# w_down in seven block products for eight: all four column groups and all 44 tiles, with the residual read and the sums joined near the end

## The reference

```python
h = rmsnorm(x, ffn_norm[l])
gate = jnp.einsum('bsd,df->bsf', h, w_gate[l])
up = jnp.einsum('bsd,df->bsf', h, w_up[l])
x = x + jnp.einsum('bsf,fd->bsd', jax.nn.silu(gate) * up, w_down[l])
return rmsnorm(x, final_norm)
```

## Time and profile before

| | us |
|---|---|
| median of 3 runs | 1979.49 |
| lowest and highest run | 1979.39, 1980.06 |
| span of the profiled execution | 1977.3 |
| first matmul of w_down | 1512.65 |
| last matmul starts | 1969.47 |

### The profile page before, as it was taken

One profiled execution on the slowest core, in us unless ns is written; L12 is line 12 of the kernel. 1 busy time (PEld: TensorE's weight loads), 2 busy tenths in 40 slices (PEclk: granted clock), 3 DMA queues, 4 the chain that ended last, 5 costly groups with the idle time before them and its releaser, 6 DMA issues.

```text
span 1977.3 us, 29282 instructions
## 1 busy us (share of the span) xinstructions
PE 1967.3 (99%) x10300; PEld 1691.6 (86%) x10300; DVE 1654.7 (84%) x2386; ACT 1126.6 (57%) x2064; POOL 167.2 (8%) x261
## 2 busy tenths in 40 slices
PE   9999999999999999999999999999999999999998
PEld 7888888888888988888888888888888888888886
DVE  8877767777766999999999999999998688697886
ACT  6566666666346655555646555555556355566643
POOL 5002333223100000000000000000000000000000
PEclk9999999999999999999999999999999999999999
DMA  9322222224334344443434344444347836546433
GB/s 343 127 83 70 70 71 70 69 70 139 102 117 138 119 148 137 130 139 130 137 132 142 131 134 135 136 139 135 132 138 238 303 120 227 176 148 221 126 130 133
DMA packets 132889, 276.16 MB, mean 140 GB/s; under 512 B 13392, under 2 KB 13424, under 8 KB 131744
## 3 DMA queue, kind: packets, MB, share of 16 engines
q1 hardware_dynamic: 120896, 239.65, 37.9%
q0 software_dynamic: 6640, 23.82, 3.1%
q10 hardware_dynamic: 5232, 11.04, 1.6%
HBM read 242.99 MB, written 31.46 MB: 139 GB/s over the span
## 4 chain that ended last, share of the span: by engine, by line
PE 96%; DVE 2%; issue 1%; DMA 1%; ACT 0%; SPq 0%; POOLq 0%; POOL 0%; DVEq 0%; ACTq 0%
PE bank L841 25%; PE bank L844 13%; PE bank L702 7%; PE bank L768 7%; PE bank L770 7%; PE bank L769 7%; PE bank L704 7%; PE bank L703 7%; PE bank L900 3%; PE bank L898 3%; PE bank L899 3%; PE bank L925 2%; PE bank L942 1%; PE bank L910 1%; PE bank L909 1%
## 5 line engine op out<-in xcount | busy, mean ns | idle before, releaser
L841 PE MATMUL bank<-s_two,t_hi 128*128 128x512 f32 x2352 | 557.3, 390 | 0.0
L1485 ACT ACTIVATE t_hi<-t_raw 128x1792 fp32r<-128x1792 f32 x176 | 302.5, 1720 | 358.1 <-DVE t_raw L2155 269.7
L841 PEld LDWEIGHTS bank<-s_two,t_hi 128*128 128x128 f32 x2352 | 433.5, 188 | 84.7
L2161 DVE TENSOR_TENSOR t_lo<-t_raw,t_hi 128x1792 fp32r<-128x1792 f32 x176 | 355.7, 2021 | 20.7 <-ACT t_hi L1485 20.6
L844 PEld LDWEIGHTS bank<-s_two,t_lo 128*128 128x128 f32 x2352 | 298.9, 191 | 10.4 <-DVE t_lo L2161 0.6
L844 PE MATMUL bank<-s_two,t_lo 128*128 128x256 f32 x2352 | 302.1, 283 | 0.4 <-DVE t_lo L2161 0.4
L1136 ACT ACTIVATE w_hi<-raw 128x512 fp32r<-128x512 f32 x268 | 168.8, 631 | 189.5 <-PE bank L770 141.4
L1778 DVE TENSOR_TENSOR w_lo<-raw,w_hi 128x512 fp32r<-128x512 f32 x268 | 184.6, 690 | 56.6 <-ACT w_hi L1136 56.0
L2152 DVE TENSOR_TENSOR t_raw<-t_raw 128x1024 f32<-128x1024 f32 x176 | 215.0, 1221 | 17.2 <-DMA t_raw<-in_w_gu 15.5
L702 PE MATMUL bank<-h_hi,w_hi 128*128 128x512 f32 x416 | 166.0, 399 | 1.1 <-DVE h_lo L1782 0.6
L704 PE MATMUL bank<-h_lo,w_hi 128*128 128x512 f32 x416 | 162.6, 391 | 0.0
(11 more groups left out here) (260 smaller groups left out, 3487.8 us busy)
## 6 DMA issues: line engine op xcount, KB each, us to landing
t_raw<-in_w_gu SPq DMA_DIRECT2D x348, 256.0 KB, 2.8
raw<-in_w_down SPq DMA_DIRECT2D x112, 256.0 KB, 3.6
raw<-in_w_in SPq DMA_DIRECT2D x104, 256.0 KB, 2.7
gu_mid<-part POOLq DMA_DIRECT2D x43, 512.0 KB, 2.9
gu_next<-gu_mid SPq DMA_DIRECT2D x36, 512.0 KB, 6.9
raw<-in_w_out SPq DMA_DIRECT2D x64, 256.0 KB, 3.0
fast_y<-in_w_down SPq DMA_DIRECT2D x24, 512.0 KB, 5.0
fast_z<-in_w_down SPq DMA_DIRECT2D x16, 512.0 KB, 4.7
```

Source lines behind the costliest of these rows:

```text
L841: mm = nc.tensor.matmul(b[:, :], t_hi[r][:, ti, q, :], both, start=d == 0 and q == 0, stop=d == DOUBLES - 1 and q == 1 and i < 4, skip_gro ...
L1485: nc.scalar.activation(t_hi[r][:, :, :, :].rearrange("p a q c -> p (a q c)"), t_raw[r][:, 1:8, :, :].rearrange("p a q c -> p (a q c)"), AC ...
L2161: nc.vector.tensor_tensor(t_lo[r][:, :, :, :].rearrange("p a q c -> p (a q c)"), t_raw[r][:, 1:8, :, :].rearrange("p a q c -> p (a q c)"), ...
```

## The change

All of w_down now goes by seven block products. There are two pairs of column groups: (0, 2) with h = 0 and (1, 3) with h = 1. Chunk 0 has 4 tiles (2 near, 2 far) and chunks 1 to 5 have 8, together 44. A unit is (chunk c, product p, depth u, pair h), 256 rows by 512 columns and 12 matmuls as before; a chunk has 7 x 2 x 2 = 28 units, chunk 0 has 14. The order of the products is P1, P5, P6, P7, P3, P4, P2.

- Removed: the plain units, their splits on ACT and DVE, their adds to `x_res`, the last 4 tiles' part.
- Every product's sums stay in `m_sum`, now 14 buffers for 7; a product takes four banks, and `keep` and `seed` move four.
- The high and low parts of weights have rings of 4 (before 2): ACT may start `f_high` of the unit three ahead when unit v-1 is off the banks' list (`f_used`).
- DVE's loop does, for unit v: `f_sum` of v+4, gate operations of the next chunk (slots of `GATE_SLOT`), `f_low` of v+3.
- SP reads z again in P3, after `f_low` of the same unit, and P4's `f_sum` takes it.
- The residual is read in chunk 5, at P3's first unit, into the place where gate tiles lay; joins and adds follow in `ending`.
- The last product, P2 of chunk 5, is done pair by pair, and the last pair by position block. Rows 256 to 511 are finished first.

```diff
-CHUNK = 8
-CHUNKS = (TILES - 4) // CHUNK
...
+P1, P5, P6, P7, P3, P4, P2 = range(FAST)
+SUMMED_W, SUMMED_A = (P5, P6, P7, P4), (P5, P6, P7, P3)
+FAST_FROM = "yxxyzxz"
+CHUNKS = 6
+ENDING = CHUNKS - 1
+DEPTHS = (1,) + (2,) * ENDING
+F_RING, A_RING = 4, 4
+F_AHEAD, SUM_AHEAD = 3, 4
...
+GATE_SLOT = ({4: 2, 5: 3, 6: 4, 7: 5, 0: 6, 1: 7, 2: 8, 3: 9}, {4: 4, 5: 6, 6: 8, 7: 10, 0: 14, 1: 16, 2: 18, 3: 20})
...
+            if p == P3:
+                sp.wait_ge(f_lo_done, v + 1)
+                load_block("z", c, u, h, 1, 0)
...
+            if (c, p, u, h) == (ENDING, P3, 0, 0):
...
+                for n in range(NC):
+                    sp.wait_ge(x_moved[n], X_SPILLED)
+                    sp.dma_start(x_res[:, :, 512 * n:512 * (n + 1)],
...
+            if v >= F_RING:
+                act.wait_ge(f_used, v - F_RING + 1)
+            nc.scalar.activation(flat(f_hi[v % F_RING]), flat(fast_raw[FAST_FROM[p], u][h]), ACT.Copy).then_inc(f_hi_done, 1)
...
         silu(0, 0)
         silu(0, 1)
...
+        act.wait_ge(t_used, ALL_T - 2)
+        f_high(0)
+        f_high(1)
+        act.wait_ge(t_lo_done, ALL_T)
+        a_high(ITEMS[0])
+        silu(0, 4)
+        silu(0, 5)
         take_products(7, 1, 0, 5)
...
+            if e == 20:
+                for h in range(2):
+                    dve.wait_ge(joined, h + 7)
+                    add_block(sum_of(P5, h), 1, h + 2, r2_sign, 0)
...
+        def fast_slot(v):
+
+            c, e = UNITS[v][0], v - FIRST_UNIT[UNITS[v][0]]
+            if v + SUM_AHEAD < len(UNITS):
+                f_sum(v + SUM_AHEAD)
+                for item in items_at(v + SUM_AHEAD):
+                    a_sum(item)
+            if c < ENDING:
+                for k, slot in GATE_SLOT[c > 0].items():
+                    if e == slot:
+                        gate_scaled(c + 1, k)
+                    if e == slot + 2:
+                        gate_times_up(c + 1, k)
+            if v + F_AHEAD < len(UNITS):
+                f_low(v + F_AHEAD)
+                for item in items_at(v + F_AHEAD):
+                    a_low(item)
+            if v == 1:
+                post(7, 1)
+            if c == ENDING:
+                ending(e)
```

More of the change, by code:

```diff
@@ L256, in build @@
[L256 to L269, removed]
+    place_d = place_s
+    g_near = sb("g_near", [P, 4, 2, SEQ], at=place_d)
@@ new lines, in build @@
+    g_far = [sb(f"g_far{i}", [P, 4, 2, SEQ], at=place_d + 16384 * (i + 1)) for i in range(2)]
+    x_res = sb("x_res", [P, NT, D], at=place_d)
+    places_f = (place_w + 8192, place_w + 16384, place_s4 + 16384, place_s4 + 24576)
+    f_hi = [sb(f"f_hi{r}", [P, 2, SEQ], F32R, at=at) for r, at in enumerate(places_f)]
+    f_lo = [sb(f"f_lo{r}", [P, 2, SEQ], F32R, at=at + 4096) for r, at in enumerate(places_f)]
+    places_a = [place_x + 24576 + 4096 * r for r in (2, 3, 0, 1)]
+    a_hi = [sb(f"a_hi{r}", [P, 2, HALF], F32R, at=at) for r, at in enumerate(places_a)]
@@ L418, in unit_of @@
[L418 to L451, removed]
+    def a_source(c, p, u):
+        near, far = g_near[:, 2 * u:2 * u + 2, 0, :], g_far[c % 2][:, 2 * u:2 * u + 2, 0, :]
+        if p == P1:
+            return near[:, :, 0:HALF]
+        if p == P4:
+            return far[:, :, HALF:SEQ]
+        if p == P2:
+            return far[:, :, 0:HALF]
+        return g_far[c % 2][:, 2 * u + (p == P7), 1, :].rearrange("p (k c) -> p k c", c=HALF)
@@ new lines, in fast_unit @@
+        def fast_unit(v, halves=range(2)):
+            c, p, u, h = UNITS[v]
+            if 0 in halves:
+                pe.wait_ge(f_lo_done, v + 1)
+                pe.wait_ge(a_lo_done, ITEM[c, p, u] + 1)
+                if u == 0 and c > 0:
+                    pe.wait_ge(seeded, seeded_count(c, p, h))
+                elif u == 0 and p == P1:
+                    pe.wait_ge(bank_taken, taken_by(0, TILES - 2) + 4 * (h + 1))
+                elif u == 0 and p == P5:
+                    pe.wait_ge(bank_taken, taken_by(0, TILES - 1))
+                elif u == 0:
+                    pe.wait_ge(kept, kept_count(c, p - 2, h))
+            rf, ra = v % F_RING, ITEM[c, p, u] % A_RING
+            for tp in halves:
+                for i in range(2):
+                    ah, al = a_hi[ra][:, i, P * tp:P * (tp + 1)], a_lo[ra][:, i, P * tp:P * (tp + 1)]
+                    mm = three(bank_of(c, p, h, tp)[:, :], ah, al, f_hi[rf][:, i, :], f_lo[rf][:, i, :],
+                               c == 0 and i == 0, u == DEPTHS[c] - 1 and i == 1)
+            return mm
@@ L1738, in _ @@
+        f_high(2)
+        a_high(ITEMS[1])
         take_products(7, 1, 5, QUAD)
[L1739 to L1751 removed]
@@ L2534, in _ @@
[L2534 to L2541 removed]
+        f_low(0)
@@ new lines, in _, with gain @@
+        a_low(ITEMS[0])
+        gate_scaled(0, 4)
+        gate_scaled(0, 5)
+        f_low(1)
+        gate_times_up(0, 4)
+        gate_times_up(0, 5)
+        f_sum(2)
+        a_sum(ITEMS[1])
+        f_sum(3)
+        f_low(2)
+        a_low(ITEMS[1])
+        for v in range(len(UNITS) - 2):
+            fast_slot(v)
+        def gain(n):
+            cols = slice(512 * n, 512 * (n + 1))
+            nc.vector.tensor_tensor(o_fin[:, n, :], x_res[:, 1, cols], g_fin[:, cols], ALU.mult).then_inc(gained, 1)
@@ L2544, in _ @@
+        finish_mean(0, 7, 5, 3)
+        dve.wait_ge(added, C11_LEFT + 4)
+        gain(1)
+        dve.wait_ge(sq_done, FIRST_SQ + 16 + 8)
+        dve.wait_ge(total_done, 7)
+        nc.vector.tensor_scalar(mean[:, 1:2], sums[:, 1, 2:3], 1.0 / D, mean_rest[:, 0:1], ALU.mult, ALU.add).then_inc(mean_done, 1)
+        for i in range(2):
+            finish_row(0, slice(1024 * i, 1024 * (i + 1)), 6)
     @block.gpsimd
```

855 lines of the change are left out of this document (320 added, 535 removed).

## The result

| | before | after |
|---|---|---|
| median of the runs, us | 1979.55 | 2032.64 |
| lowest and highest run | 1979.39, 1980.06 | 2032.09, 2033.90 |
| span of the profiled execution | 1977.3 | 2030.3 |
| first matmul of w_down | 1512.65 | 1515.76 |
| end of the last matmul | 1969.86 | 2010.86 |

The ratio is 1.0269 (95% interval 1.0256 to 1.0282). The sign and the cause were forecast; the loss was forecast at 33.5 us and is 53, outside the range.

A forecast was written before the change was run, and what follows sets the result against it. DVE was taken to become the bound of w_down, 433 us for PE's 419. 1977.3 - 38.1 + 19.3 (chunk 0) + 21.7 (chunks 1 to 4) + 16.2 (chunk 5) + 14.5 (end) = 2010.9, with 2.2 for the median 2013; range 1992 to 2024.

The forecast's parts named there:

- Which engine bounds: w_down stage: DVE has 433 us of work for PE's 419, so DVE bounds even without waits.
- Rivals A: w_down stage: PE stays the bound, 1941, or 1949 with DVE's sum as the limit; chance 0.04.
- rival B: w_down stage: DVE bounds but reads land in time, 1987, half of it 1965 to 1995; chance 0.15.
- signs named: w_down: DVE 90% or more; three PE idles over 5 us in first 55; f_hi waiting at chunk ends.
- Start: w_down's first unit: starts at 1514.2, after copies out of the last gate tile's banks, a 1.6 us term.
- large terms: Chunk 0: PE stalls of 5.6, 5.7 and 5.2 us, from DVE's early work and late z reads.
- small terms: Chunk 0: three slots carry 2.9 to 3.5 us of DVE work for 2.72, 1.2 us more.
- rival D: As the forecast, but the clock falls in long stalls or x_res is slower: 2018 to 2028; chance 0.21.
- Chunks 1 to 4: PE stalls 7.6 us in chunk 1, then 4.7 each: 2.6 early slots, 1.4 later slots and z, 0.7 signals.
- Chunk 5: 16.2 us of PE stall: DVE waits 6.8 for z behind residual reads, then has 32.3 of work.
- The tail: After the last matmul: DVE's list and output writes, end 21.6 us after PE, 14.5 more than before.
- lower end of the mechanism: All reads landing at once takes 8.8 off chunk 0, 5.3 chunks 1 to 4, 6.8 chunk 5, 5 end: 1985.

The follow-up runs named there:

- z early: Changed kernel with y and z swapping roles, P4's far block read four units sooner, the gain's read moved: 1994.55 us, ratio 1.0074.
- spread: On z early, gate operations moved to slots 12 to 15 and 18 to 22, the last gate tile's post to unit 8: 1982.27 us.
- the earlier start: On the post split, gate operations of chunk 0's far tiles put ahead of its first low parts, silus likewise: 1979.74 us.
- the post split: On spread, the last gate tile's post cut in two, at units 8 and 11: 1979.85 us, ratio 1.0004.
- half reads: Changed kernel with only gate, not up, read for the near tiles of chunks 2 to 5: 2020.92 us, ratio 1.0212.
- The residual read behind z: Changed kernel with the four residual reads issued after P3's last z read instead of its first: 2025.95 us, ratio 1.0237.

## Why the prediction was wrong, step by step

- **Which engine bounds: right.** Rivals A and B fell. PE's 168 matmuls less were right, DVE's durations too (73.4 us of work in a chunk for 72.8). Three of the signs named did not come: DVE was busy 86% and not 90%, PE sat for over 5 us twice in the first 55 us and not three times (5.2, 5.5, then 2.4), and `f_hi` waited for PE only twice in the stage (4.2 us), not at each chunk's end.
- **Start.** 1.5 us later than forecast, but DVE's last low part of the gate stage already began at 1505.12 for 1503.74, before anything that was changed. That was no part of the change.
- **Chunk 0: right in its large terms**, within 0.2 us each, as were its z waits, less closely (5.5 and 3.7 for 4.9 and 3.9). The small terms, 1.2, came out at 3.8. 1.6 of them are PE running slowly after the first long stall. PE as it resumes after the first long stall:

```profile
1534.87 0.79 PE L702 MATMUL bank<-f_hi,a_hi 128*128 128x512 f32 x1 [5.20 <-DVE f_lo L1688]
1535.45 0.63 PE L703 MATMUL bank<-f_hi,a_lo 128*128 128x512 f32 x1
1535.88 0.63 PE L704 MATMUL bank<-f_lo,a_hi 128*128 128x512 f32 x1
1536.31 0.63 PE L702 MATMUL bank<-f_hi,a_hi 128*128 128x512 f32 x1
...
1538.44 0.49 PE L704 MATMUL bank<-f_lo,a_hi 128*128 128x512 f32 x1
```

The starts are 0.43 us apart for 0.227, and the windows give the level:

```profile
1537.00:1538.00 1.00, 1.00 (x3) 0.72 (x3) 1.00 (x2) 1.00 (x4) 0.00 (x0) 0.50 0.00 0
...
1539.00:1540.00 1.00, 1.00 (x6) 0.81 (x5) 1.00 (x2) 1.00 (x2) 0.00 (x0) 1.00 0.93 260
```

  The clock is at 1.2 GHz when PE resumes and back at 2.4 GHz 4 us later. In the stage some 70 matmuls ran so, which makes 14 us of PE time more. I had taken nothing and kept 8 us for the range: rival D was right that it happens. The Trainium skill (TensorE: Matmul & The Clock Gate, Part 1) says that throttled is the default state and activity releases it; the trace agrees inside the stage too, not only at its end.

  Much of it cost nothing. The third "stall" of chunk 0, 5.2 us, is a unit whose twelve matmuls all ran slowly (2.4 us more) and then 2.4 us of idleness: PE would have waited for that low part in any case. At the end of chunk 5, seven or eight of the last 36 matmuls ran at 0.43 us in some versions and none in others. The slow ones lose 1.6 more in chunk 5 and 1.6 less in the tail: chunk 5 and tail are 11.3 and 19.4 with z early, spread, and with the earlier start, 9.7 and 21.0 with the post split, each time 30.7 together. DVE's list sets the end. In the middle it may have cost a little: chunk 2, without slow matmuls, lost 7.6, chunks 3 and 4, with eight each, 8.3, on z waits of 4.7, 5.0 and 5.0. For the rest of the 14 us the price stays open.
- **Chunks 1 to 4: the step that failed.** "the z read takes most of what slots 12 to 15 gave back (it lands 2.2 us after DVE wants it, being behind three other reads), 1.4". It lands 4.7 us after in chunk 2, 4.8 to 5.0 in the others. Landing of z's reads in chunk 2:

```profile
  DVE fast_x L2213: 4.7, 1
...
DMA to landing us min/median/max: 7.8/7.9/9.2
```

  When z is issued at 1704.27, five reads are still out. Of these the second landed at 1706.02; at 1.3 us for each of the next three and z, z would be there at 1711.2, 2.4 after DVE wants it and so close to the forecast. But the next y read landed 3.5 us after the one before it, while the queue moved 211 and 262 GB/s for two microseconds where it moves 400:

```profile
1705.00:1706.00 1.00, 1.00 (x7) 0.80 (x6) 1.00 (x3) 1.00 (x3) 0.00 (x0) 1.00 0.73 211
1706.00:1707.00 1.00, 1.00 (x6) 0.85 (x5) 0.97 (x2) 1.00 (x2) 0.00 (x0) 1.00 0.98 262
1707.00:1708.00 1.00, 1.00 (x6) 0.82 (x5) 1.00 (x1) 1.00 (x3) 0.00 (x0) 1.00 1.00 387
```

  It does so at this place in chunks 1 and 4 and in other versions too (3.3 and 3.6 us; 3.4 with the post split, 3.7 with half reads); in chunk 3 two y reads there took 2.5 and 2.6. Why is not known; nothing I ran separates it. The price was then missed as well: with the lead gone, 2.5 to 2.8 us more of wait cost PE 2.9 to 3.6 a chunk, 10.1 over the three, half of the whole miss. The forecast had 1.4 for slots 12 to 19 and z together; by "z read early", which takes 4.0 to 4.8 off each of these chunks, z alone was that much.
- **Chunk 5: right in kind, 6.7 too small.** DVE waited 11.5 for z, not 6.8. Of the 4.7, 2.5 are the gain's 1 MB read on ACT's queue, which I did not count (the longest wait is 9.0 without it); the other 2.2 no run separates. From the late z on, DVE's list to the last low part took 32.4 us (1972.4 to 2004.8) for 32.3. Another 1.6 of the 6.7 are the slow matmuls at the end, which the tail gives back. The forecast's 6.8 for z and the 6.7 won by "The residual read behind z" are not the same quantity and agree by luck: there an 11.5 us wait went and 4.0 came back as a wait for the residual.
- **The tail: 19.4 for 22.** 1.6 of the 2.6 less is the late last matmul told above. DVE's list is as forecast: from its last add of P4's banks to the last write it takes 15.2 us (2010.1 to 2025.3) for 15.4. The end of DVE and ACT; they answer to the earlier trace rows.

```profile
2014.57 2.34 DVE L2362 SCALAR_TENSOR_TENSOR x_res<-x_res,inv,g_fin 128x2048 f32<-128x2048 f32 x1
2014.73 2.59 POOL L2402 TENSOR_TENSOR inv<-mean,half 128x1 f32<-128x1 f32 x1 [0.25 <-DVE mean L2357]
...
2017.49 2.34 DVE L2362 SCALAR_TENSOR_TENSOR x_res<-x_res,inv,g_fin 128x2048 f32<-128x2048 f32 x1
...
2022.03 2.48 DVE L2362 SCALAR_TENSOR_TENSOR x_res<-x_res,inv,g_fin 128x1024 f32<-128x1024 f32 x2 [0.28 <-POOL inv L2402]
...
2025.30 0.34 ACTq L1671 DMA_DIRECT2D out_x<-x_res  x1
```

  The last write is issued 14.4 us after the last matmul, forecast 16.3; it is 5.0 from there to the end, forecast 5.3.
- **The range.** Its upper end, 2024, let the waits' errors stand by themselves. They are not independent: every late read falls on a lead that is already spent, so all of them add with the same sign. The lower end of the mechanism, 1985, does not come out of its own terms either: 1939.2 + 8.8 + 5.3 + 6.8 + 5 is 1965. With z in time the kernel took 1994.6, for rival B's 1987. The sum of the misses: start 1.5, chunk 0 2.3, chunk 1 1.5, chunks 2 to 4 10.1, chunk 5 6.7, tail -2.6: 19.5.

## What to carry over

When work moves from a full engine to one with 22% idle, ask how far ahead the second may run, and draw that lead up slot by slot with everything that eats it, late reads included: once it is spent each further wait costs nearly its whole length (z's wait of 4.2 to 5.0 us cost PE 1.2 with the lead and 4.0 to 4.8 without). Count for a read all bytes queued on all queues at its issue. And place work by slot before adding or removing any: the same DVE operations in another order, with z's and the gain's reads moved, took 50 of the 53 us back.
